# Delta-rule scan in pairs of PSUM banks: one subtraction and one copy for each direction and level, VectorE's other pieces behind the subtraction, and the state's decay on GpSimd

## The chip, the cores and the metric

One core of a Trainium2 chip runs the whole kernel. The metric is the device time of one execution in microseconds (us), lower is better. All data are float32.

## The reference

Two layers of a hybrid trunk over 256 context and 512 latent tokens, width 1024. Each layer projects its normed input, runs three groups of heads (latent attention, a gated delta rule in both directions, pooling), projects back, and then runs an expert-choice mixture of 16 experts. The change lies in the gated delta rule: 4 heads of 128, in two directions.

```python
def gated_delta_chunked(q, k, v, g, beta, s0):
    # chunked: S_t = a_t S_{t-1}(I - b_t k_t k_t^T) + b_t k_t v_t^T, o_t = S_t^T q_t
    gc = jnp.cumsum(chunks(g), axis=-1)
    decay = jnp.exp(jnp.where(incl, gc[..., :, None] - gc[..., None, :], -jnp.inf))
    kb = kc * bc[..., None]
    a_low = jnp.where(strict, jnp.einsum('nbhcd,nbhsd->nbhcs', kb, kc) * decay, 0.0)
    tmat = a_low + jnp.eye(C, dtype=f32)
    w = lax.linalg.triangular_solve(tmat, kb * jnp.exp(gc)[..., None], left_side=True, lower=True, unit_diagonal=True)
    u = lax.linalg.triangular_solve(tmat, vc * bc[..., None], left_side=True, lower=True, unit_diagonal=True)
    qk = jnp.einsum('nbhcd,nbhsd->nbhcs', qc, kc) * decay
    def step(s, inp):
        v_new = u_i - jnp.einsum('bhcd,bhde->bhce', w_i, s)
        o = jnp.einsum('bhcd,bhde->bhce', qg_i, s) + jnp.einsum('bhcs,bhse->bhce', qk_i, v_new)
        s = s * jnp.exp(gl_i)[..., None, None] + jnp.einsum('bhcd,bhce->bhde', kd_i, v_new)
        return s, o
    s_final, o = lax.scan(step, s0.astype(f32), (w, u, qk, qg, kd, g_last))
    ...
```

The decayed state, `s * exp(gl)`, plus the product of a chunk's keys and new values is the state for the next chunk. The triangular solve with `tmat` is what takes the levels below.

## The kernel before

Both layers have the same stages: input projection, attention, the scan of the delta rule (which the change touches), output projection, router, experts. Five engines run their own programs and meet at semaphores: TensorE (`pe`), VectorE (`dve`), ScalarE (`act`), GpSimd (`pool`), and SyncE for the weights' DMAs.

**The scan.** The 768 tokens are six tiles of 128 (`NT`); step `j` (0 to 5) takes tile `j` of the forward direction (`d` = 0) and a tile from the other end for the backward one (`d` = 1), with all four heads. The inverse of a head's 128x128 triangular matrix is built by doubling: after the first blocks (`diagonal_blocks`, L874, and `inverse_of_blocks`, L2226) come five levels `n` = 1 to 5. A level is a chain through three engines:

- `level_factor` (L896): 32 matmuls of 64x64 for both directions, into two banks. Bank `zo` has heads 0 and 1 of both directions, `zd` heads 2 and 3. Both are announced after the last matmuls of direction 1.
- VectorE subtracts each bank from the identity into `gW` (L2288, two instructions of 128x256).
- `level_update` (L914), once for each direction: 32 matmuls into two banks, `x` and `xb`.
- ScalarE copies each of the four banks into the ring's `gXC` (L1795, four instructions of 128x256). The next level's factor reads them; its first matmuls need only `xb` of direction 0.

GpSimd masks the factors' weights for the levels ahead (L2606, L2607, each group counted in the semaphore `ml`).

**The pieces between.** The rest of the rule fills the time in which a level waits. `BETWEEN` gives the pieces of each of 13 slots; TensorE runs slot 2n-1 between factor and update of level n, and slot 2n behind the update:

```python
BETWEEN = (
    (("wt", 0), ("wt", 1)), (("v", 0), ("v", 1)), (("go", 0),), (("go", 1),), (("st", 0), ("st", 1)),
    (("g", 0),), (("g", 1),), (), (("kk", 0),), (("kv", 0),), (("kk", 1), ("qk", 0)), (("qk", 1),), (("kv", 1),))
```

`wt`, `v`, `go`, `st` finish step j-1 (new values, output, state); `g`, `kk`, `qk` prepare step j+1; `kv` transposes the keys and values of step j (`kr` and `vr`, L815, L816). On TensorE `kk` is L807, `qk` L810, `wt` L821, `v` L831 and L833, `go` L844 and L845, `st` L849, and `g` has nothing. VectorE takes their products out of PSUM in its own program order: both subtractions of level n, then slot 2n-1, then slot 2n. So a piece of slot 2n (`st` of slot 4, `kk` of slot 8) stands ahead of the subtractions of level n+1. `st` is four instructions for each direction (L2206: state times decay plus product), `kk` six (L2168 to L2172), `kv` three (L2182, L2183, L2188), and `g` three (L2155 to L2159). In layer 1 `go` and `qk` are left out for context tiles (steps 0 and 1).

In layer 0 TensorE also makes the modulation of both layers in this stage: six loads (`ar`) in each step. One load's first half (L547) is in an even slot, its second half (L547, then L531) in the next odd slot, just ahead of the update. It keeps one bank from the one to the other, and ScalarE empties it (L1498, L1492).

**The banks.** PSUM has eight banks. `claim` takes the next one in a circle and makes TensorE wait there until its last product was read out; `claim_two` takes two neighbours, does not start at bank 7, and skips banks that are held. A claim stands at the head of a group of matmuls, so everything behind it on TensorE waits too:

```python
while turn[0] % BANKS == BANKS - 1 or turn[0] % BANKS in held or (turn[0] + 1) % BANKS in held:
    turn[0] += 1
b = turn[0] % BANKS
turn[0] += 2
for x in (b, b + 1):
    bank_unused(x)
```

With one bank for each claim, a level of the kernel before takes six banks.

## Time and profile before

| | |
|---|---|
| three timed runs | 1947.01, 1946.89, 1941.97 us; median 1946.89 |
| profiled execution | 1942.07 us, its span 1939.9 us, granted clock 0.977 |
| TensorE busy | 1833.6 us, 95% of the span |
| scan of layer 0 (382 to 616 us) | 234.0 us, TensorE busy 224.24 |
| scan of layer 1 (1386 to 1572 us) | 186.0 us, TensorE busy 154.61 |

Everything but the two scans is untouched. The two scans together are 420 of 1939.9 us. In the views, "PE" is TensorE's matmuls, "DVE" VectorE, "ACT" ScalarE, "POOL" GpSimd. The chain of waits lists what came last, piece after piece in order of time; in it a piece of TensorE lasts until the next one's results begin to come, so a start there can lie some 0.07 us behind the instruction's own.

In the rows by stretch the columns are: stretch, its length, then busy us (x instructions) of PE, PEld (weight load), DVE, ACT and POOL, the granted clock, the DMA engines' busy share, and GB/s.

### The profile page before, as it was taken

The numbers are of one execution on the slowest core, as the hardware profiler recorded it, in microseconds if no ns is written. First come the engines' busy times: TensorE is split into PE (matmuls) and PEld (weight loads), VectorE is DVE, ScalarE is ACT, GpSimd is POOL, SyncE is SP. The second block draws the span as 40 slices with busy tenths as digits, with TensorE's granted clock in tenths as the row PEclk, the third lists the DMA queues.
The fourth block names the chain that finished last, engine by engine and source line by source line (L and its number), as shares of the span: only waits on it lengthen the run. The fifth ranks groups of instructions, "written<-read, shape, count | busy, mean of one in ns | idle before, by whom it ended". The sixth has DMA issues, their size and how long they took to land.

```text
span 1939.9 us, 41539 instructions
## 1 busy us (share of the span) xinstructions
PE 1833.6 (95%) x17621; PEld 1150.2 (59%) x17621; DVE 729.0 (38%) x1523; ACT 500.7 (26%) x1133; POOL 376.8 (19%) x506
## 2 busy tenths in 40 slices
PE   6999999999999998999999999999888899999998
PEld 4565556677787554565556445556577764455454
DVE  3145333444553335111121425334465632522323
ACT  3212532343332223001111231353433221200010
POOL 1612000244452001310011032200254610100000
PEclk7999999999999999999999999999899999999999
DMA  9410000164555316889998412000300022499996
GB/s 323 142 57 22 22 1 1 47 212 154 181 172 163 136 44 233 307 330 366 359 364 312 148 44 66 22 0 1 99 14 25 13 89 74 173 411 411 410 411 253
DMA packets 139545, 320.67 MB, mean 165 GB/s; under 512 B 10760, under 2 KB 97582, under 8 KB 124046
## 3 DMA queue, kind: packets, MB, share of 16 engines
q1 hardware_dynamic: 127584, 287.20, 40.0%
q0 software_dynamic: 6432, 20.00, 3.7%
q10 hardware_dynamic: 5390, 11.44, 1.7%
q8 instruction: 110, 1.80, 0.4%
q14 instruction: 29, 0.24, 0.0%
HBM read 305.45 MB, written 13.16 MB: 164 GB/s over the span
## 4 chain that ended last, share of the span: by engine, by line
PE 84%; DVE 6%; issue 4%; ACT 3%; DMA 2%; SPq 1%; POOL 0%; ACTq 0%; DVEq 0%; POOLq 0%
PE psum L610 17%; PE psum L1143 11%; PE psum L1045 7%; PE psum L1174 6%; PE psum L730 3%; PE psum L1152 3%; PE psum L914 3%; PE psum L1224 3%; PE psum L547 2%; PE psum L751 2%; PE psum L896 2%; PE psum L1186 2%; PE psum L807 1%; PE psum L531 1%; PE psum L831 1%
## 5 line engine op out<-in xcount | busy, mean ns | idle before, releaser
L610 PE MATMUL psum<-hT,ring 128*128 128x256 f32 (+2 forms) x976 | 337.7, 503 | 4.3 <-ACT hT L1518 3.8
L610 PEld LDWEIGHTS psum<-hT,ring 128*128 128x128 f32 (+1 forms) x976 | 184.4, 191 | 145.3 <-issue 127.6
L1143 PE MATMUL psum<-ring,arena 128*64 128x256 f32 x1536 | 174.9, 384 | 5.8 <-issue 2.0
L1143 PEld LDWEIGHTS psum<-ring,arena 128*64 128x64 f32 x1536 | 111.1, 138 | 66.6 <-issue 17.4
L1045 PE MATMUL psum<-hT,ring 128*128 128x512 f32 (+1 forms) x384 | 139.4, 521 | 0.9 <-DVE xT L2323 0.9
L2410 DVE TENSOR_TENSOR arena<-arena,psum 128x384 f32<-128x384 f32 (+1 forms) x32 | 15.6, 488 | 260.7 <-PE psum L1152 161.6
L1045 PEld LDWEIGHTS psum<-hT,ring 128*128 128x128 f32 x384 | 72.7, 190 | 64.8 <-issue 61.5
L914 PE MATMUL psum<-wbuf,ring 64*64 64x64 f32 x1920 | 78.4, 229 | 31.3 <-DVE wbuf L2288 25.6
L1795 ACT COPY ring<-psum 128x256 f32<-128x256 f32 x240 | 73.4, 383 | 97.4 <-PE psum L914 97.4
L914 PEld LDWEIGHTS psum<-wbuf,ring 64*64 64x64 f32 x1920 | 68.9, 141 | 37.9 <-issue 35.8
L2717 POOL DMA_INDIRECT big<-h_rows_lat,idx x16 | 15.7, 979 | 381.7 <-PE psum L1248 173.7
L2439 DVE SCALAR_TENSOR_TENSOR xT<-psum,modraw,xT 128x512 f32<-128x512 f32 (+1 forms) x136 | 79.7, 622 | 21.2 <-PE psum L1224 15.1
L730 PE MATMUL psum<-hT,ring 128*128 128x256 f32 (+1 forms) x192 | 82.0, 537 | 0.0
L1863 ACT COPY arena<-psum 128x512 f32<-128x512 f32 (+2 forms) x49 | 23.6, 482 | 220.5 <-PE psum L1165 147.2
L914 PE MATMUL psum<-ring,wbuf 64*64 64x64 f32 x1920 | 75.8, 229 | 0.6 <-issue 0.6
L2067 DVE SCALAR_TENSOR_TENSOR big<-psum,cols,big 128x511 f32<-128x511 f32 (+1 forms) x44 | 27.6, 628 | 125.9 <-ACT big L1619 124.9
L1224 PE MATMUL psum<-arena 128*128 128x512 f32 x144 | 65.8, 602 | 4.0 <-DVE arena L2426 2.3
L1867 ACT ACTIVATE arena<-psum 128x384 f32<-128x384 f32 (+1 forms) x32 | 14.1, 439 | 213.9 <-PE psum L1152 108.6
L914 PEld LDWEIGHTS psum<-ring,wbuf 64*64 64x64 f32 x1920 | 65.0, 141 | 0.7 <-issue 0.7
L2288 DVE TENSOR_TENSOR wbuf<-lev,psum 128x256 f32<-128x256 f32 x120 | 45.1, 418 | 52.0 <-PE psum L896 51.7
L547 PE MATMUL psum<-ring,scol 128*32 128x256 f32 x768 | 64.5, 424 | 0.0
L2606 POOL TENSOR_TENSOR mlaw<-dT,lev 128x256 f32<-128x256 f32 x60 | 43.8, 730 | 104.6 <-PE psum L896 97.0
(351 smaller groups left out, 3386.7 us busy)
## 6 DMA issues: line engine op xcount, KB each, us to landing
ring<-in_moe_w_gate SPq DMA_DIRECT2D x64, 1024.0 KB, 10.9
ring<-in_ada_w SPq DMA_DIRECT2D x48, 1024.0 KB, 5.4
ring<-in_moe_w_up SPq DMA_DIRECT2D x32, 1024.0 KB, 9.1
hT<-in_moe_w_down SPq DMA_DIRECT2D x24, 1024.0 KB, 12.2
ring<-in_w_in SPq DMA_DIRECT2D x20, 1024.0 KB, 6.5
big<-in_moe_w_up SPq DMA_DIRECT2D x16, 1024.0 KB
sz<-in_moe_w_down SPq DMA_DIRECT2D x16, 1024.0 KB
big<-in_moe_w_down SPq DMA_DIRECT2D x16, 1024.0 KB, 14.4
```

The source lines that it names most:

```text
L547: m = pe.matmul(ada[1][r:r + 32, 0:SLOT_COLS], lhsT=scol[:, 2 * k:2 * k + 32], rhs=ada[2][:, k, :], start=half == 0, stop=half == 1)
L610: m = pe.matmul(b[0:c1 - c0, 0:n], lhsT=w[:, k, c0:c1], rhs=hT[:, k, t0:t0 + n], start=k == 0, stop=k == KD - 1)
L730: x = pe.matmul(b[:, 0:n], lhsT=w[:, k, m % 2 * P:(m % 2 + 1) * P], rhs=hT[:, k, t0:t0 + n], start=k == 0, stop=k == KD - 1)
L914: m = pe.matmul(bs[kind][o, i * HALF:(i + 1) * HALF], lhsT=v if transposed else w, rhs=w if transposed else v, start=True, stop=True)
L1045: m = pe.matmul(b[:, 0:x], lhsT=w[:, k, c:c + P], rhs=mixT[:, k, t0:t0 + x], start=k == OUT_REST[0], stop=k == OUT_GDN[-1])
L1143: m = pe.matmul(b[e * CAP_L:(e + 1) * CAP_L, 0:2 * P], lhsT=xs[:, k, e, 0:CAP_L], rhs=w[e][:, 2 * (k - ks[0]) + q, :], start=k == 0, stop= ...
L1152: m = pe.matmul(b[r:r + CAP_C, 2 * P:3 * P], lhsT=xs[:, k, e, CAP_L:CAP], rhs=v[:, 2 * (k % (KD // 2)) + q, f * P:(f + 1) * P], start=k == ...
L1174: m = pe.matmul(ys[c][e * CAP_L:(e + 1) * CAP_L, :], lhsT=hidT[:, q, f * P + e * CAP_L:f * P + (e + 1) * CAP_L], rhs=w[e][:, f, c * 512:(c ...
L1224: m = pe.matmul(b[:, 0:SEQ], lhsT=ylat[:, k * P:(k + 1) * P], rhs=Sl[:, :], start=True, stop=True)
L1795: read_out(act.copy(gXC[j % 2][:, d, w:w + GH, :].rearrange("p h c -> p (h c)"), b), key)
L2288: read_out(dve.tensor_tensor(gW[:, :, h0:h0 + 2, :], eyes, b, ALU.subtract), key)
L2439: read_out(dve.scalar_tensor_tensor(out=x, in0=b[:, 0:n], scalar=mods_of[l][:, 5 * KD + k, 1 - g:2 - g], in1=x, op0=ALU.mult, op1=ALU.add) ...
```

## The change

- A factor is now one group of 16 matmuls for each direction, into a pair of neighbouring banks, announced by itself (`z`). An update also goes into one pair. A level takes eight banks in place of six.
- VectorE subtracts once for each direction (still two instructions of 128x256 for a level, each over two banks). ScalarE copies once for each direction (two of 128x512 in place of four of 128x256).
- VectorE's slot 2n stands behind the subtractions of level n+1 (ahead of slot 2n+1).
- The state's decay is taken off VectorE's `st`: GpSimd multiplies the state by its decay (`decay_state`, one instruction for each direction), between the masks of level 3 and those of level 4, and signals `sdec`. VectorE then adds the product in one instruction for each direction.
- ScalarE issues the loads of the next decay rows at slots 2 and 3, one each, in place of both at slot 4.

```diff
@@ -387,6 +387,12 @@
             product_ready(eng, ("s", l, i, h))
             b = where[("s", l, i, h)][0]
             return psum[:, b:b + 2, :].rearrange("p a c -> p (a c)")[:, 0:(CT if i < CT else NT) * P]
+
+        def two_banks(eng, key):
+
+            product_ready(eng, key)
+            b = where[key][0]
+            return psum[:, b:b + 2, :]
 
         def attended(eng, l, calls, n):
 
@@ -876,34 +882,29 @@
                                 if (d, i) == (1, 1):
                                     done(m, keys[kind])
 
-                def level_factor(j, n, x):
-
-                    keys = ("zo", l, j, n), ("zd", l, j, n)
-                    bs = [claim(key) for key in keys]
-                    for d in range(2):
-                        if n > 1:
-                            evacuated(pe, ("xb", l, j, d, n - 1))
-                        elif d == 0:
-                            evacuated(pe, ("t0o", l, j))
-                            evacuated(pe, ("t0d", l, j))
-                        for i, pair in enumerate(((0, 3), (1, 2))):
-                            if i and n > 1:
-                                evacuated(pe, ("x", l, j, d, n - 1))
-                            for kind, h in enumerate(pair):
-                                c = (2 * d + h % 2) * HALF
-                                for k in range(2):
-                                    t, o = rows_of[k ^ xt_half(h, n)], rows_of[k ^ x_half(h, n)]
-                                    m = pe.matmul(bs[kind][o, c:c + HALF], lhsT=gML[n % 2][t, d, h, :],
-                                                  rhs=x[t, d, XTB[h], :], start=True, stop=True)
-                                if d and i:
-                                    done(m, keys[kind])
+                def level_factor(j, n, x, d):
+
+                    key = ("z", l, j, n, d)
+                    bs = claim_two(key).rearrange("p (a c) -> p a c", a=2)
+                    if n > 1:
+                        evacuated(pe, ("x", l, j, d, n - 1))
+                    elif d == 0:
+                        evacuated(pe, ("t0o", l, j))
+                        evacuated(pe, ("t0d", l, j))
+                    for pair in ((0, 3), (1, 2)):
+                        for kind, h in enumerate(pair):
+                            c = h % 2 * HALF
+                            for k in range(2):
+                                t, o = rows_of[k ^ xt_half(h, n)], rows_of[k ^ x_half(h, n)]
+                                m = pe.matmul(bs[o, kind, c:c + HALF], lhsT=gML[n % 2][t, d, h, :],
+                                              rhs=x[t, d, XTB[h], :], start=True, stop=True)
+                    done(m, key)
 
                 def level_update(j, n, x, d):
 
-                    keys = ("x", l, j, d, n), ("xb", l, j, d, n)
-                    bs = [claim(key) for key in keys]
-                    for kind in range(2):
-                        evacuated(pe, ("zd" if kind else "zo", l, j, n))
+                    key = ("x", l, j, d, n)
+                    bs = claim_two(key).rearrange("p (a c) -> p a c", a=2)
+                    evacuated(pe, ("z", l, j, n, d))
                     same, other = ((2, 1), (0, 0), (1, 0), (2, 0)), ((3, 0), (3, 1), (0, 1), (1, 1))
                     for i in range(GH):
                         for kind, (h, transposed) in enumerate((same[i], other[i])):
@@ -911,10 +912,9 @@
                                 a = rows_of[k ^ x_half(h, n)]
                                 o = rows_of[k ^ (xt_half(h, n + 1) if transposed else x_half(h, n + 1))]
                                 w, v = gW[a, d, h, :], x[a, d, XB[h], :]
-                                m = pe.matmul(bs[kind][o, i * HALF:(i + 1) * HALF], lhsT=v if transposed else w,
+                                m = pe.matmul(bs[o, kind, i * HALF:(i + 1) * HALF], lhsT=v if transposed else w,
                                               rhs=w if transposed else v, start=True, stop=True)
-                            if i == GH - 1:
-                                done(m, keys[kind])
+                    done(m, key)
 
                 def first_chunk(n):
 
@@ -980,7 +980,8 @@
                     gdn_between(j, 0)
                     for n in range(1, LEVELS - 1):
                         pe.wait_ge(s["ml"], (LEVELS - 1) * j + n + 1)
-                        level_factor(j, n, x)
+                        for d in range(2):
+                            level_factor(j, n, x, d)
                         gdn_between(j, 2 * n - 1)
                         if n == 1:
                             pe.wait_ge(s["x0"], j + 1)
@@ -990,7 +991,6 @@
                     keys = ("z6d", l, j), ("z6o", l, j)
                     bs = [claim(key) for key in keys]
                     for d in range(2):
-                        evacuated(pe, ("xb", l, j, d, LEVELS - 2))
                         evacuated(pe, ("x", l, j, d, LEVELS - 2))
                     for i in range(2):
                         for kind, h in enumerate((i, 2 + i)):
@@ -1722,9 +1722,8 @@
                             gdn_piece(what, i, d)
                     if slot in G_SLOTS and j + 1 < NT:
                         gdn_piece("g", j + 1, G_SLOTS.index(slot))
-                    if slot == 4 and 1 <= j < NT - 1:
-                        for d in range(2):
-                            decay_rows(j + 1, d)
+                    if slot in (2, 3) and 1 <= j < NT - 1:
+                        decay_rows(j + 1, slot - 2)
                     if l == 0 and slot % 2 and slot < 2 * ADA_CHUNK:
                         ada_out(ADA_FIRST + ADA_CHUNK * j + slot // 2)
                     if j == 0 and slot < 4:
@@ -1789,10 +1788,9 @@
                     for n in range(1, LEVELS - 1):
                         gdn_between(j, 2 * n - 1)
                         for d in range(2):
-                            for w, name in ((GH, "xb"), (0, "x")):
-                                key = (name, l, j, d, n)
-                                b = product_ready(act, key)[:, 0:GH * HALF]
-                                read_out(act.copy(gXC[j % 2][:, d, w:w + GH, :].rearrange("p h c -> p (h c)"), b), key)
+                            key = ("x", l, j, d, n)
+                            b = two_banks(act, key)[:, :, 0:GH * HALF]
+                            read_out(act.copy(gXC[j % 2][:, d, :, :].rearrange("p (a h) c -> p a (h c)", a=2), b), key)
                         gdn_between(j, 2 * n)
                     for w, name in ((0, "z6d"), (2, "z6o")):
                         key = (name, l, j)
@@ -2202,11 +2200,9 @@
                         if j == 0:
                             read_out(dve.tensor_copy(S[:, d, :, :].rearrange("p h c -> p (h c)"), b), key)
                         else:
-                            for h in range(GH):
-                                m = dve.scalar_tensor_tensor(out=S[:, d, h, :], in0=S[:, d, h, :],
-                                                             scalar=gt4[:, j % 2, d, 1, h:h + 1],
-                                                             in1=b[:, h * P:(h + 1) * P], op0=ALU.mult, op1=ALU.add)
-                            read_out(m, key)
+                            dve.wait_ge(s["sdec"], 2 * (j - 1) + d + 1)
+                            x = S[:, d, :, :].rearrange("p h c -> p (h c)")
+                            read_out(dve.tensor_tensor(x, x, b, ALU.add), key)
 
                 def gdn_between(j, slot):
 
@@ -2280,14 +2276,15 @@
                 for j in range(NT):
                     if j:
                         inverse_of_blocks(j)
-                    gdn_between(j, 0)
                     for n in range(1, LEVELS - 1):
-                        for h0, name in ((0, "zo"), (2, "zd")):
-                            key = (name, l, j, n)
-                            b = product_ready(dve, key)[:, 0:GH * HALF].rearrange("p (d h c) -> p d h c", d=2, h=2)
-                            read_out(dve.tensor_tensor(gW[:, :, h0:h0 + 2, :], eyes, b, ALU.subtract), key)
+                        for d in range(2):
+                            key = ("z", l, j, n, d)
+                            b = two_banks(dve, key)[:, :, 0:2 * HALF].rearrange("p a (h c) -> p a h c", h=2)
+                            read_out(dve.tensor_tensor(gW[:, d, :, :].rearrange("p (a h) c -> p a h c", a=2), eyes, b,
+                                                       ALU.subtract), key)
+                        gdn_between(j, 2 * n - 2)
                         gdn_between(j, 2 * n - 1)
-                        gdn_between(j, 2 * n)
+                    gdn_between(j, 2 * LEVELS - 4)
                     gdn_between(j, 2 * LEVELS - 3)
                     key = ("u6", l, j)
                     b = product_ready(dve, key)[:, 0:GH * HALF].rearrange("p (h c) -> p h c", h=GH)
@@ -2608,8 +2605,8 @@
 
                 def mask_read(j, n):
 
-                    product_ready(pool, ("zo", l, j, n))
-                    product_ready(pool, ("zd", l, j, n))
+                    for d in range(2):
+                        product_ready(pool, ("z", l, j, n, d))
 
                 def begin(j):
 
@@ -2633,6 +2630,17 @@
                     product_ready(pool, ("t0d", l, j))
                     pool.wait_ge(s["x0"], j + 1)
                     masked(2, j)
+
+                def decay_state(j):
+
+                    for d in range(2):
+                        if need_ctx or tile_of(d, j) >= CT:
+                            product_ready(pool, ("go", l, j, d))
+                        else:
+                            product_ready(pool, ("v", l, j, d))
+                        x = S[:, d, :, :]
+                        pool.tensor_tensor(x, x, gt4[:, j % 2, d, 1, :].unsqueeze(2).to_broadcast([P, GH, P]), ALU.mult
+                                           ).then_inc(s["sdec"], 1)
 
                 def queries(j):
 
@@ -2658,10 +2666,11 @@
                     for n in range(3, LEVELS - 1):
                         mask_read(j, n - 2)
                         masked(n, j)
+                        if n == 3 and j >= 2:
+                            decay_state(j - 1)
                     if j + 1 < NT:
                         decays(j + 1)
                     for d in range(2):
-                        evacuated(pool, ("xb", l, j, d, LEVELS - 2))
                         evacuated(pool, ("x", l, j, d, LEVELS - 2))
                         if j:
                             product_ready(pool, ("v", l, j - 1, d))
```

## Rows read from the trace of the kernel before

**Rows 1.** Busy time by stretch: scan of layer 0, its step 4, scan of layer 1.
```profile
382.00:616.00 234.00, 224.24 (x4673) 176.85 (x4672) 115.64 (x276) 88.08 (x264) 100.64 (x129) 0.97 0.57 184
...
541.66:581.23 39.57, 38.86 (x812) 31.48 (x816) 21.14 (x53) 13.76 (x44) 18.25 (x24) 1.00 0.54 176
...
1386.00:1572.00 186.00, 154.61 (x3864) 138.12 (x3861) 108.78 (x266) 70.09 (x192) 91.57 (x119) 0.95 0.09 28
```

**Rows 2.** Waits in the scan of layer 1: total us, times, longest.
```profile
PE psum L914 <- DVE wbuf L2288: 24.4, 21, 1.6
```

**Rows 3.** Waits in the scan of layer 0.
```profile
PE psum L914 <- issue: 5.9, 5, 2.8
```

**Rows 4.** Chain of waits, layer 1, step 5: levels 3 to 4. Start, us, what.
```profile
1563.23 1.16 PE psum L914 x64
...
1564.53 1.09 PE psum L896 x30
...
1565.64 0.76 DVE wbuf L2288 x2
...
1566.54 1.16 PE psum L914 x64
```

**Rows 5.** Timeline of ScalarE, layer 1, step 5, level 3.
```profile
1564.01 1.20 ACT L1795 COPY ring<-psum 128x256 f32<-128x256 f32 x4 [4.04 <-PE psum L914]
```

**Rows 6.** Timeline of VectorE, layer 1, step 3, levels 3 to 5.
```profile
1493.46 2.16 DVE L2206 SCALAR_TENSOR_TENSOR arena<-arena,small,psum 128x128 f32<-128x128 f32 x8 [1.49 <-PE psum L849]
1495.54 0.75 DVE L2288 TENSOR_TENSOR wbuf<-lev,psum 128x256 f32<-128x256 f32 x2
...
1502.03 0.42 DVE L2168 TENSOR_TENSOR dT<-psum,arena 64x256 f32<-64x256 f32 x1 [2.43 <-PE psum L807]
...
1504.30 0.75 DVE L2288 TENSOR_TENSOR wbuf<-lev,psum 128x256 f32<-128x256 f32 x2
```

**Rows 7.** Chain of waits, layer 1, step 3: `st`, factor 3, and from update 4 on.
```profile
1492.34 1.98 PE psum L849 x16
1494.32 0.69 PE psum L896 x31
...
1499.74 1.16 PE psum L914 x64
...
1505.20 1.16 PE psum L914 x64
```

**Rows 8.** Chain of waits, layer 0, step 4: levels 1, 2, 3 and 5.
```profile
550.33 1.27 PE psum L914 x64
...
557.87 1.09 PE psum L914 x64
...
561.51 0.62 PE psum L896 x32
...
563.24 1.09 PE psum L914 x64
...
564.90 0.71 issue
...
570.22 0.83 PE psum L896 x32
...
573.18 1.27 PE psum L914 x64
```

**Rows 9.** Timeline of ScalarE, layer 0, step 4.
```profile
543.41 0.60 ACT L1707 ACTIVATE arena<-psum 128x512 f32<-128x512 f32 x1 [2.91 <-PE psum L821]
...
550.64 0.17 ACT L1492 COPY modraw<-psum 128x4 f32<-128x4 f32 x1
```

**Rows 10.** Timeline of VectorE, layer 0, step 4.
```profile
542.78 0.68 DVE L2188 TENSOR_TENSOR arena<-psum,small 128x512 f32<-128x512 f32 x1
```

**Rows 11.** Groups by line in the scan of layer 1: busy us, mean ns; idle before.
```profile
L1795 ACT COPY ring<-psum 128x256 f32<-128x256 f32 x120 | 36.2, 385 | 83.4 <-PE psum L914 83.4
...
L2585 POOL TENSOR_TENSOR arena<-arena,small 128x512 f32<-128x512 f32 x10 | 10.4, 1041 | 29.3 <-ACT arena L1704 29.3
```

More of the change, by code:

```diff
@@ L338, in build_program @@
                  "lmul", "egc", "xg", "dex", "eb", "dm", "x0", "xd", "away", "ml", "qg", "osq", "mixd", "rmax",
-                 "rexp", "aff", "top", "hrow", "att", "tok", "idx", "gath", "grow", "gr0", "gr1", "cur", "scat", "arow", "S", "dve", "pool_e"]
+                 "rexp", "aff", "top", "hrow", "att", "tok", "idx", "gath", "sdec", "grow", "gr0", "gr1", "cur", "scat", "arow", "S", "dve", "pool_e"]
         FIRST_ALONE = ("zero", "zrow", "scat", "arow")
```

## The prediction

> **What bounds the kernel now.** I read the page's busy time, then busy time by stretch, then in both scans the chain of waits and the timelines of each engine, and last I followed the claims of PSUM banks through the code.
>
> The reader should see two different stages under one code. In layer 0 the scan lasts 234.0 us and TensorE is busy for 224.24 of them; in its step 4 it is 38.86 of 39.57 [rows 1]. The loads of the modulation and the pieces fill every wait of a level, so a shorter chain through VectorE and ScalarE gains next to nothing there, and each new wait of TensorE is paid in full. In layer 1, without those loads, it is busy for 154.61 of 186.0 us [rows 1], and 24.4 us of its idle time end with VectorE's subtraction [rows 2]. Only there can the change gain.
>
> **A level that nothing fills** (layer 1). From update 3 to update 4 of step 5 it is 1566.54 - 1563.23 = 3.31 us [rows 4]: copies begin 0.78 behind the update's start [rows 4, 5], the factor goes on until the last copy is out (1.09 in place of 0.69 [rows 4, 7]), two subtractions take 0.76, and 0.14 passes to TensorE [rows 4]. With the change, S being the update's start: half an update is 0.54 of 1.09 us [rows 8], so direction 0 is still ready at S+0.78. Its one copy of 128x512 takes 0.60, the time of a ScalarE read of this size [rows 9]; factor 0 starts at S+1.52, 16 matmuls are 0.31 (half of 0.62 [rows 8]) and ready at about S+2.0, one subtraction is 0.42, update 0 starts at S+2.56. Direction 1 is copied by S+1.92, its factor ends at S+2.37, its subtraction at about S+2.95, just in time behind update 0. Gain 0.75 us.
>
> The wide copy itself gains little: the four narrow ones take 1.20 together [rows 5] though one takes 385 ns [rows 11], so they overlap and two take some 0.65, against 0.60. The Trainium skill (VectorE: DVE Perf Modes, The TRN2 errata) gives ScalarE a fixed cost for each instruction, 172 cycles at 1.2 GHz out of PSUM, paid once by a large tile; by it a merged pair would save an estimated 0.14 us at each of the about nine levels on the path of layer 1, so 1.3 us more than I forecast. The rows agree with its duration of one instruction, not with a saving in a row of them.
>
> **What the banks do.** This is the part on which the sign hangs. A level now takes 8 of 8 banks, before 6. Following both kernels' claims in program order: before, no claim meets a bank whose user is fewer than seven claims back. Now these meet young ones, each at the head of TensorE's queue:
> - update 5, direction 0, takes the bank of `kk` of slot 8 (steps 0 to 4, both layers), which VectorE now reads behind both subtractions;
> - update 3 takes the banks of `st` (steps 1 to 5), also read behind them. In layer 1 direction 1 waits for both. In layer 0 direction 0 waits for both in steps 2, 3 and 5, where bank 7 is skipped, and the directions for one each in steps 1 and 4;
> - in layer 0 updates 1 and 5 (direction 0) take the bank of the load that TensorE ended just ahead of them; update 2 so in steps 2 and 5, and its direction 1 in steps 0, 1, 4; direction 1 of update 4 in all, of update 3 in step 0.
>
> **Layer 1, step 3, summed.** Factor 3 starts at 1494.32 [rows 7]. Before, eight instructions of `st` of 2.16 us stand ahead of the subtractions, which begin at 1495.54 [rows 6]. Now: subtractions from about 1494.8 to 1495.5, then two adds of 0.68 [rows 10] that overlap a little, to 1496.7. Update 3, direction 1, starts at 1496.85 (direction 0 is long done), its copy is out at 1498.23, its factor at 1498.7, its subtraction at 1499.3, so update 4 ends at 1499.99, against 1499.74 + 1.09 = 1500.83 before [rows 7, 8]. 0.84 gained. `kk` follows on TensorE. Factor 5 starts at 1501.1, the subtractions end at 1502.3, then `kk` on VectorE, 1504.30 - 1502.03 = 2.25 [rows 6], then the bank: update 5 at 1504.67 against 1505.20 [rows 7]. So 0.53 is left, and VectorE, busy from there to the step's end, hands on the same 0.53. Steps 1 and 2 have no `go` behind update 1, hence one unfilled level more: 0.53 + 0.75 = 1.3 each. Step 4: 0.53. Step 5 has no `kk`, and 0.8 stays; its last level is filled by `kv`. Step 0, where ScalarE's gates hold the first levels, about 1.0. Sum 1.0 + 2.6 + 1.1 + 0.8 = **5.5 us gained** in layer 1.
>
> **Layer 0, summed**, on step 4's rows.
> - Update 1: the load's last read-out ends at 550.81 [rows 9]; with 0.14 direction 0 starts at 550.95, not 550.33. Before, only the last bank of direction 1 was shared with the load, and the update took 1.27, not 1.09 [rows 8]: that proves the kind of wait and its price of 0.18, which goes. Net 0.5, steps 1 to 5: 2.5.
> - Update 2: 0.7 in steps 2 and 5, 0.16 where it is direction 1 (three): 1.9.
> - Update 3: factor at 561.51 [rows 8], the first subtraction at 561.9, the second ends 562.7, adds until 563.9, start 564.03, not 563.17: 0.86 in three steps; 0.3 in steps 1 and 4, 0.16 in step 0: 3.4.
> - Update 4: 0.16 six times: 1.0.
> - Update 5: factor at 570.22 [rows 8], subtractions until 571.4, `kk` 2.25 to 573.6, start 573.74, end 574.83, before 573.18 + 1.27 = 574.45 with its start counted 0.07 late: 0.45 five times, and 0.5 for the load in step 5: 2.8.
>
> Together 11.6 us. Not all adds: TensorE already stands without cause in the semaphores, 5.9 us in updates [rows 3], 0.71 once ahead of factor 4 [rows 8]. A stop may take such a stall's place. I take 2 us off; the bounds are 0 and 8 (5.9 and some more of the 234.0 - 224.24 us idle). **9.6 us lost.**
>
> **Costed at nothing.** VectorE saves 2.16 - 1.3 us of `st` in each step; in layer 1 this is in the sum, in layer 0 also. GpSimd's two decays are 1.04 each by the same form [rows 11] and wait for `go` of slot 3; behind them stand the masks of level 4, two instructions of half that size, for which factor 4 waits. `go` ends as update 2 begins, 1492.34 - 1.09 = 1491.25, and update 4 starts at 1499.74 [rows 7, 8], factor 4 some 2 us ahead of it: 6.4 us of room for 2.1 + 1.0. `st` on VectorE waits for `sdec`; its product comes 1.09 + 1.98 = 3.1 us behind `go`'s [rows 7, 8]. Without this cover each microsecond would be paid in five steps. The decay rows' loads go earlier on ScalarE, some 0.4 us of issue each, and wait for `go`, which is done before update 2's copies: nothing. Two-bank reads on either engine: nothing, bound 0.05 us for each on the path, some 2 us.
>
> **Sum.** 9.6 - 5.5 = +4.1 us. On the profiled execution's 1942.07 (span 1939.9) this is 1946.2. That execution lies 4.8 below the median of the runs, 1946.89, two of which stand within 0.12 of each other. On the median: **1951.0 us**.
>
> **Rivals.**
> - *The waits of layer 0 cost nothing.* If its pace is set by what TensorE's sequencer waits for without a semaphore [rows 3], stops merely take the place of those stalls. With all 9.8 us of idle time [rows 1] as cover: 11.6 - 9.8 - 5.5 = -3.7, 1943.2. Against it: update 1's 1.27 [rows 8], where a shared bank was paid in full. It decides the sign from 11.6 - 5.5 = 6.1 us absorbed.
> - *Faster, by the shorter level.* If the subtraction ahead of the pieces is worth the whole of its wait in layer 1, as it is where no bank is shared, then of the 24.4 us that end with it [rows 2] about half go (0.75 of each 1.5), 12 us, while layer 0, spared by the same, keeps the load's waits, 2.5 + 1.9 + 1.0 = 5.4: 5.4 - 12 = -6.6, 1940.3. It needs `kk` and `st` out of their banks before updates 5 and 3, though VectorE starts them later than before. It decides from a layer 1 that gains more than layer 0 loses.
> - *The stops feed on each other.* ScalarE's `g` activations (three of 128x512, so 1.8 us [rows 9]) then stand ahead of the load's read-out and of the copies of level 4, another 0.5 us in ten steps, with nothing absorbed: 11.6 + 5 - 5.5 = +11, 1958.
> - *GpSimd's masks come late.* If `decay_state` holds factor 4: over 3 us of cover must go; 1 us in eight steps is +8 on the forecast, 1959.
>
> **Chances.** Forecast (0 to +8 us) 0.52; waits absorbed (-6 to 0) 0.20; faster by over 6 us 0.10; stops feed on each other 0.14; masks 0.04. The likeliest one's own range is 1947 to 1955. The range for 8 in 10 reaches into both sides: 1940 to 1959. 0.3% is 5.8 us, about what a measurement of this kernel can tell from no change: faster 0.13, same 0.50, slower 0.37.
>
> **What would show it.** Right: the scan of layer 0 some 8 to 10 us longer with TensorE's busy time the same, stops of 0.5 to 0.9 ahead of updates 1, 3 and 5, the last two ended by VectorE's `st` and `kk`; the scan of layer 1 some 5 shorter, an unfilled level at 2.6 us; the idle time ended by L2288 well below 24.4. Wrong: layer 0 unchanged, or `ml` waits ahead of factor 4.

## The result, and the profile after

The changed kernel takes 1953.57 us (median of 6 runs, 1951.23 to 1959.29), the kernel before, timed beside it, 1945.61 (6 runs, 1936.59 to 1947.01). The ratio, estimated from all runs, is 1.0058, with a 95% interval of [1.0043, 1.0074], so 8 to 14 us slower; the two medians alone are 8.0 us apart, a quotient of 1.0041. The predicted 1951.0 and its range hold, but the loss is over the 0.3% that a measurement can tell, to which I gave 0.37 against 0.50 for no change. The profiled execution's span is 1950.0 us against 1939.9: 10.1 more, where the forecast was 4.1.

In the changed kernel's lines, L899 is the factor, L915 the update, L2283 the subtraction, L1793 the copy, L2166 to L2170 `kk` on VectorE, L2205 `st`'s add, L553 and L537 the modulation's load, L1492 its read-out. First, busy time by stretch, both whole scans (from their first factor to the output projection), before the change:

```profile
385.32:626.12 240.80, 230.90 (x4745) 184.87 (x4742) 117.53 (x278) 86.79 (x265) 99.69 (x129) 0.97 0.55 179
1389.36:1585.25 195.89, 163.89 (x3953) 148.46 (x3953) 112.18 (x270) 70.22 (x194) 93.16 (x123) 0.95 0.07 23
```

and after it:

```profile
382.07:636.94 254.87, 230.98 (x4744) 183.30 (x4741) 114.38 (x254) 82.72 (x205) 107.65 (x137) 0.97 0.52 169
1402.89:1595.61 192.72, 161.88 (x3953) 145.92 (x3953) 109.50 (x246) 66.94 (x134) 101.50 (x131) 0.96 0.07 24
```

Layer 0 is 14.1 us longer with TensorE's busy time unchanged (230.90 and 230.98): all of it is standing still. Layer 1 is 3.2 shorter. The stages around the scans differ by -3.2, +2.7 and -0.3. TensorE's waits in layer 0, which answer to [rows 3]:

```profile
PE psum L915 <- issue: 12.4, 11, 2.8
PE psum L915 <- ACT modraw L1492: 3.6, 5, 0.7
PE psum L915 <- DVE ring L2170: 3.2, 5, 0.7
PE psum L915 <- DVE arena L2205: 2.3, 3, 0.8
PE psum L553 <- issue: 1.3, 1, 1.3
```

The main bank waits foretold are there: the load's read-out ahead of update 1 in five steps, `kk` ahead of update 5 in five, `st` ahead of update 3 in steps 2, 3 and 5. The first row was not foretold: "issue" in updates, a stop for which the trace names no semaphore, has doubled from [rows 3]. Six of its eleven stops are of 0.9 us or more, 10.3 us in all. The other five are of 0.57 or 0.18 us, 2.1 us in all, and each ends 0.09 or 0.10 us behind a read-out of the load's bank or of `st`, at places foretold ahead of updates 2, 3 and 5. They are bank waits as well. Layer 1, to be held against [rows 2]:

```profile
PE psum L915 <- DVE ring L2170: 7.0, 4, 1.8
PE psum L899 <- ACT ring L1793: 6.6, 10, 2.0
PE psum L915 <- issue: 3.8, 4, 1.7
PE psum L915 <- DVE wbuf L2283: 3.6, 12, 0.6
PE psum L915 <- DVE arena L2205: 3.1, 4, 0.8
```

The subtraction's 24.4 us have shrunk to 3.6, yet only 3.2 us came out: `kk`'s and `st`'s banks took much of the place. The fifth wait for `kk`'s bank, in step 1, is in the "issue" row (1.71 us, ending 0.10 behind `kk`'s last read-out), and the factors now wait 6.6 us for ScalarE's copies, 1.6 before. The chain of waits of layer 1's step 3, to be held against [rows 7] (start, us, what):

```profile
1505.39 0.44 PE psum L899 x15
...
1506.52 0.69 DVE arena L2205
...
1507.89 0.73 PE psum L915 x31
...
1512.25 0.43 PE psum L899 x15
...
1515.32 0.30 DVE ring L2170
...
1515.66 1.16 PE psum L915 x64
```

From factor 3, the update starts 2.50 us later (I had 2.53), factor 5 is 6.86 later (6.78), update 5 10.27 (10.35; before 10.88). VectorE's timeline there answers to [rows 6]:

```profile
1505.85 0.75 DVE L2283 TENSOR_TENSOR wbuf<-lev,psum 128x256 f32<-128x256 f32 x2 [2.80 <-PE psum L899]
1506.52 1.28 DVE L2205 TENSOR_TENSOR arena<-arena,psum 128x512 f32<-128x512 f32 x2
...
1512.70 0.75 DVE L2283 TENSOR_TENSOR wbuf<-lev,psum 128x256 f32<-128x256 f32 x2 [1.63 <-PE psum L899]
1513.38 0.41 DVE L2166 TENSOR_TENSOR dT<-psum,arena 64x256 f32<-64x256 f32 x1
```

`st` went from 2.16 to 1.28 us, but stands between subtraction and update, whose bank it frees. The unfilled level of step 5, in the chain, answers to [rows 4]:

```profile
1575.85 0.73 PE psum L915 x31
1576.58 0.02 issue
1576.60 0.59 ACT ring L1793
...
1577.33 0.50 PE psum L899 x16
...
1577.85 0.43 DVE wbuf L2283
...
1578.41 0.59 PE psum L915 x25
```

1578.41 - 1575.85 = 2.56 us from update to update, against 3.31 before. This looks like the 2.56 forecast, but both rows are of direction 1, which `st`'s bank had held back; the forecast was of direction 0, whose updates start at 1574.36 and 1577.58, 3.22 apart. A level as short as forecast shows only in e3 below (2.49). Layer 0's step 4, to be held against [rows 8]:

```profile
551.71 0.07 ACT modraw L1492
551.78 0.25 issue
552.03 1.16 PE psum L915 x64
...
571.62 0.38 PE psum L899 x12
...
575.03 0.30 DVE ring L2170
575.33 0.04 issue
575.38 1.16 PE psum L915 x64
...
579.08 1.34 issue
580.42 0.59 PE psum L553 x2
```

Update 1 waits for the load's read-out, update 5 for `kk`, 3.76 us behind factor 5's start (2.96 before, 3.52 foretold; where nothing else disturbs the step it is 3.49, and 2.75 or 2.76 before). Then TensorE stands 1.34 us inside a load with no semaphore named.

### The profile page after: what moved, and what is told of

The parts are those of the page before. It is cut to its first block, busy times and chain, and to the rows that moved or that the text cites. A ratio compares the mean times of both kernels' runs of the same rounds, so it can differ in the third digit from the quotient of the medians.

```text
span 1950.0 us, 41394 instructions
## 1 busy us (share of the span) xinstructions
PE 1824.5 (94%) x17621; PEld 1140.5 (58%) x17621; DVE 723.1 (37%) x1475; ACT 492.8 (25%) x1013; POOL 392.6 (20%) x522
## 4 chain that ended last, share of the span: by engine, by line
PE 82%; DVE 7%; issue 4%; ACT 3%; DMA 3%; SPq 1%; POOL 0%; ACTq 0%; DVEq 0%; POOLq 0%
PE psum L616 17%; PE psum L1143 11%; PE psum L1045 7%; PE psum L1174 5%; PE psum L915 3%; PE psum L736 3%; PE psum L1152 3%; PE psum L1224 3%; PE psum L757 2%; PE psum L553 2%; PE psum L899 2%; PE psum L1186 2%; PE psum L813 1%; PE psum L837 1%; PE psum L789 1%
## 5 line engine op out<-in xcount | busy, mean ns | idle before, releaser
L915 PE MATMUL psum<-wbuf,ring 64*64 64x64 f32 x1920 | 78.7, 228 | 38.4 <-issue 14.2
L2283 DVE TENSOR_TENSOR wbuf<-lev,psum 128x256 f32<-128x256 f32 x120 | 46.6, 419 | 160.5 <-PE psum L899 160.2
L1793 ACT COPY ring<-psum 128x512 f32<-128x512 f32 x120 | 66.4, 587 | 112.2 <-PE psum L915 112.0
L915 PEld LDWEIGHTS psum<-wbuf,ring 64*64 64x64 f32 x1920 | 68.4, 139 | 43.3 <-issue 23.3
L2436 DVE SCALAR_TENSOR_TENSOR xT<-psum,modraw,xT 128x512 f32<-128x512 f32 (+1 forms) x136 | 79.7, 620 | 21.2 <-PE psum L1224 14.1
L915 PE MATMUL psum<-ring,wbuf 64*64 64x64 f32 x1920 | 76.4, 228 | 2.0 <-issue 2.0
L915 PEld LDWEIGHTS psum<-ring,wbuf 64*64 64x64 f32 x1920 | 64.9, 139 | 5.2 <-issue 5.2
L553 PE MATMUL psum<-ring,scol 128*32 128x256 f32 x768 | 62.5, 407 | 5.2 <-DMA ring<-in_ada_w 3.6
L2112 DVE TENSOR_REDUCE small<-psum 128x1 f32<-128x768 f32 (+1 forms) x40 | 33.8, 850 | 80.5 <-PE psum L757 80.3
```

Source lines behind the costliest of these rows:

```text
L553: m = pe.matmul(ada[1][r:r + 32, 0:SLOT_COLS], lhsT=scol[:, 2 * k:2 * k + 32], rhs=ada[2][:, k, :], start=half == 0, stop=half == 1)
L915: m = pe.matmul(bs[o, kind, i * HALF:(i + 1) * HALF], lhsT=v if transposed else w, rhs=w if transposed else v, start=True, stop=True)
L1793: read_out(act.copy(gXC[j % 2][:, d, :, :].rearrange("p (a h) c -> p a (h c)", a=2), b), key)
L2283: read_out(dve.tensor_tensor(gW[:, d, :, :].rearrange("p (a h) c -> p a h c", a=2), eyes, b, ALU.subtract), key)
L2436: read_out(dve.scalar_tensor_tensor(out=x, in0=b[:, 0:n], scalar=mods_of[l][:, 5 * KD + k, 1 - g:2 - g], in1=x, op0=ALU.mult, op1=ALU.add) ...
```

## The experiments

The changed kernel was timed beside before (1945.61). Of the experiments, the first four ran on one chip (before: 1940.47 us, median of 29 runs), the next four on a second (1939.95, 17 runs), the last three on a third (1944.59, 11 runs). Scan lengths are from one execution of each; the ratios are estimated from all runs and differ a little from the quotients of the medians.

| kernel | median us | ratio to before, 95% | layer 0 | layer 1 |
|---|---|---|---|---|
| before | | 1 | 240.8 | 195.9 |
| changed | 1953.57 | 1.0058 [1.0043, 1.0074] | 254.9 | 192.7 |
| e1 pairs only | 1944.07 | 1.0014 [0.9995, 1.0032] | 255.3 | 185.2 |
| e2 order, decay only | 1937.20 | 0.9983 [0.9967, 0.9999] | 243.3 | 193.3 |
| e3 in place | 1916.90 | 0.9882 [0.9856, 0.9909] | 231.3 | 182.3 |
| e4 changed, old order | 1938.56 | 0.9991 [0.9970, 1.0011] | 251.5 | 185.1 |
| e5 changed, 128 waits | 1951.19 | 1.0050 [1.0034, 1.0066] | 249.5 | 194.8 |
| e6 in place, old order | 1918.62 | 0.9885 [0.9861, 0.9908] | 236.9 | 181.9 |
| e7 in place, pairs only | 1923.57 | 0.9919 [0.9897, 0.9941] | 233.4 | 185.0 |
| e8 before, 128 waits | 1935.85 (1 run) | | 238.9 | 196.4 |
| e9 in place, `kk` first | 1928.86 | 0.9919 [0.9898, 0.9941] | 235.6 | 186.8 |
| e10 changed again | 1954.35 (1 run) | | 252.7 | 196.2 |
| e11 changed, 64 waits | 1955.99 (1 run) | | 257.6 | 194.8 |

**e1, the pairs alone.** VectorE's order, `st` of four instructions and the place of the decay rows' loads as before the change:

```diff
+                    gdn_between(j, 0)
                     for n in range(1, LEVELS - 1):
...
-                        gdn_between(j, 2 * n - 2)
                         gdn_between(j, 2 * n - 1)
-                    gdn_between(j, 2 * LEVELS - 4)
+                        gdn_between(j, 2 * n)
...
-                        if n == 3 and j >= 2:
-                            decay_state(j - 1)
```

> Only the bank pairs (one subtraction and one copy for each direction); VectorE's order, the four-instruction st and the decay rows' loads as before. My theory (young banks in TensorE's claims cost layer 0; the level itself is shorter in layer 1): layer 0's scan is 8 to 10 us longer, by stops ahead of updates 1, 2 and 5 that end with the read-out of the modulation load, none that end with st or kk; layer 1's scan 6 to 8 us shorter; the ratio to before 0.999 to 1.003. Rival (the reordering is what costs): ratio under 0.998, layer 0 within 3 us of before.

Layer 0's loss is the pairs' own (+14.5, where I had 8 to 10), but layer 1 gains 10.7 (I had 6 to 8), far more than with the whole change: without the new order the trace names no wait on `kk` or `st` in either layer.

**e2, order and decay alone**, on banks by twos of a level's halves as before:

```diff
-                    gdn_between(j, 0)
                     for n in range(1, LEVELS - 1):
...
+                        gdn_between(j, 2 * n - 2)
                         gdn_between(j, 2 * n - 1)
-                        gdn_between(j, 2 * n)
+                    gdn_between(j, 2 * LEVELS - 4)
```

> Only VectorE's pieces behind the subtraction, the decay on GpSimd and the earlier loads of the decay rows; one bank for each claim, as before. My theory: layer 0's scan within 2 us of before, layer 1's 2 to 4 us shorter (update 3 some 0.5 us sooner in five steps, update 5 not, since its direction 1 takes kk's bank); ratio 0.997 to 1.000. Rival (the reordering or GpSimd's decay is what costs): layer 0 some 5 us longer or more, ratio over 1.002.

It is a little faster than before (layer 0 is 2.5 us longer, layer 1 2.6 shorter). The halves alone give +0.14 and -0.17%, together +0.58: what they lose together is neither's own. In layer 1 TensorE stands 1.39 or 1.40 us at one place of each of five steps, 7.0 us in all, for which the trace names no semaphore. The place tells the cause:

```profile
1503.32 0.29 DVE L2171 TENSOR_TENSOR ring<-psum,arena 64x128 f32<-64x128 f32 x1
...
1503.72 0.27 PE L914 MATMUL psum<-wbuf,ring 64*64 64x64 f32 x2 [1.39 <-issue]
```

It is update 5 between its two directions, and in all five steps it goes on 0.10 us behind the end of `kk`'s last read-out: the wait for `kk`'s bank that the expectation names. In layer 1 it costs nothing over the kernel before, which stands 1.56 or 1.57 us for the subtraction ahead of the same update in steps 1 to 4: from factor 5 to the next step it is 12.57 us here and 12.59 before.

**e3, the update in the bank pair of its own factor.** Four banks a level in place of eight, everything else as changed. The factor of a direction has been read when its update begins, so the wait is one that the update has anyway.

```diff
                     key = ("x", l, j, d, n)
-                    bs = claim_two(key).rearrange("p (a c) -> p a c", a=2)
                     evacuated(pe, ("z", l, j, n, d))
+                    b0 = where[("z", l, j, n, d)][0]
...
+                    where[key] = (b0, uses[b0], 0)
+                    uses[b0] += 1
+                    second_of[b0 + 1] = (b0, uses[b0])
+                    bs = psum[:, b0:b0 + 2, :]
```

> The changed kernel, but an update takes the pair of banks of its own direction's factor, whose read-out it waits for anyway, so a level takes four banks in place of eight. My theory (the new waits are all of banks): no stop of an update ends with st, kk or a load's read-out, layer 0's scan is within 3 us of before, layer 1's some 12 us shorter, ratio to before 0.992 to 0.995. Rival (order, decay or wide reads cost, whatever the banks): layer 0 stays 8 us or more over before, ratio 1.000 or more.

The banks were the loss, and the gain is larger than expected: 1.2% faster than before. Every wait on `st` and on the load's read-out is gone; of those on `kk` 1.1 us is left in layer 1. Its stretches:

```profile
385.72:617.04 231.32, 225.71 (x4745) 181.18 (x4741) 113.89 (x254) 82.55 (x205) 107.66 (x137) 0.99 0.58 186
1380.13:1562.40 182.27, 159.80 (x3954) 144.28 (x3954) 108.58 (x247) 66.58 (x134) 101.13 (x131) 0.98 0.08 25
```

Layer 0 is 9.5 us under before. In place the load's bank is shared with no update any more (9.14 from factor 1 to factor 2, before 9.32; 10.62 from factor 5 on, before 10.80), some 2 us in all; the rest goes with less standing still (5.6 us against 9.9) and a clock granted at 0.99, not 0.97.

**e4, the changed kernel with VectorE's old order** (the diff of e1 without its last two lines).

> The changed kernel with VectorE's order of before (slot 2n ahead of the subtractions of level n+1); pairs, decay on GpSimd and earlier loads stay. My theory: stops that end with st go, update 5 waits for the load alone; layer 0's scan 8 to 10 us over before, layer 1's 7 to 9 under it, ratio 0.998 to 1.002, so 0.4% better than the changed kernel. Rival (the order gains, as it is meant to): slower than the changed kernel, ratio 1.008 or more.

It is as fast as before and by the ratios 0.67% faster than the change. With eight banks a level, the new order, made to shorten the level, costs more than it gives: TensorE waits 9.4 us for the subtraction in place of 3.6, but no longer for `kk` and `st`.

```profile
PE psum L915 <- DVE wbuf L2284: 9.4, 15, 1.2
PE psum L899 <- ACT ring L1793: 4.3, 7, 2.0
PE psum L915 <- issue: 1.9, 2, 1.4
```

**e6 and e7, the same two on top of the in-place banks.** e6 is e3 with the old order, e7 is e3 with all of e1's diff.

> The in-place kernel (update in the bank pair of its own direction's factor, four banks a level) with VectorE's pieces in their old order around the subtraction. Theory A (the new order is harmful only by holding kk's and st's banks, which nobody young waits for any more with four banks a level): the new order is then worth its price in layer 1, so this kernel is slower than the in-place one by 2 to 5 us there, ratio to before about 0.990. Theory B (the new order gains nothing even so, because the old pieces fitted beside the level): the same as the in-place kernel within 1.5 us, ratio about 0.988.

> The bank pairs alone, in place: VectorE's old order, the state's decay in VectorE's st as before the change, decay rows loaded at the old place. Against the pairs alone with eight banks a level (255.3 us of scan in layer 0, 185.2 in layer 1). Theory A (bank waits are all that the pairs cost): scan of layer 0 at 231 to 236, of layer 1 at 182 to 184, ratio to before 0.988 to 0.991, so the order and GpSimd's decay are worth nothing measurable together. Theory B (in place needs the new order, since the subtraction is what the level waits for): layer 1 at 187 or more, ratio 0.992 or more. Also: GpSimd's masks ended 6.4 us of waits of the diagonal blocks in layer 1 of the in-place kernel; if its two decays of 1.04 us each are the cause, these waits are near 1.5 us here.

e6 equals e3 by the ratio: once no claim meets a young bank, one whose product was claimed just ahead, the order is worth nothing measurable in either direction (Theory B there). e7 falls between its two theories. It is 0.34% slower than e6 by the ratios, whose intervals overlap a little (0.26% by the medians, on one chip); layer 1, by 3.1 us, agrees: an `st` of 2.16 us in place of 1.28 ahead of the subtraction makes factor 3 to factor 4 3.25 us in place of 2.67 in four steps. So GpSimd's decay seems to gain there; the place of the decay rows' loads, which e7 changes too, was not tried alone. The waits for GpSimd ahead of the diagonal blocks, 6.4 us in e3, are 1.3 us in e7, but also in e6, with the decay on GpSimd: the decay is not their cause.

**e9, `kk` of direction 1 ahead of `kv` on VectorE**, on e3:

```diff
                         gdn_between(j, 2 * n - 2)
+                        if n == LEVELS - 2 and j + 1 < NT:
+                            gdn_piece("kk", j + 1, 1)
                         gdn_between(j, 2 * n - 1)
-                    gdn_between(j, 2 * LEVELS - 4)
+                    if j + 1 < NT:
+                        gdn_piece("qk", j + 1, 0)
```

> The in-place kernel with VectorE's kk of direction 1 ahead of kv of direction 0, nothing else. In layer 1 of the in-place kernel the levels are down to 2.49 us, but 6.4 us of TensorE's waits (five of some 1.3) end with GpSimd's mask ahead of the diagonal blocks, and those masks wait for kk of direction 1, which VectorE begins 1.15 us late behind three instructions of kv of 0.68 each. Theory A (this queue is the end of a step): the five waits fall to 0.3 or so each, the scan of layer 1 from 182.3 to 177 to 179 us, the ratio to before 0.985 to 0.987. Theory B (VectorE as a whole bounds the step, so the order of its pieces moves the wait elsewhere): scan of layer 1 at 181 to 183, ratio as the in-place kernel's, 0.988.

Neither theory held: the ratio is 0.9919, and layer 1 grew to 186.8 us. 1.4 of the 4.5 us between it and e3 is a stop of the kind below, in step 1. The waits moved. The three largest of e3 in layer 1, then the three that are new in e9 (its waits for ScalarE's copies are 6.4 us, for the subtraction 3.4):

```profile
PE psum L899 <- ACT ring L1798: 7.5, 10, 2.7
PE psum L880 <- POOL mlaw L2609: 6.4, 5, 2.6
PE psum L920 <- DVE wbuf L2288: 3.3, 12, 0.6
```

```profile
PE psum L827 <- DVE ring L2301: 3.3, 5, 0.8
PE psum L821 <- DVE arena L2186: 2.5, 4, 0.6
PE psum L880 <- DVE arena L2191: 1.6, 1, 1.6
```

GpSimd's masks no longer end a wait, VectorE's other pieces do. The reason can be read in e3's own chain, which from the end of step 3 into step 4 runs on VectorE for 9.0 us (1485.49 to 1494.51) with no other engine in it:

```profile
1485.83 0.69 DVE arena L2185
1486.52 0.60 DVE arena L2186
1487.12 0.60 DVE arena L2191
1487.72 0.32 DVE dT L2171
...
1489.87 1.27 DVE arena L2180 x2
```

So in the in-place kernel VectorE's queue sets the end of a step of layer 1, and there a shorter level, now 2.49 us, should not help.

**e5, e8, e10 and e11: the stops that no semaphore ends.** The "issue" rows needed a cause. Here is the longest, the chain of the changed kernel in layer 0's step 0, and then the DMA queues of the same kernel from 396.5 to 397.7 us (packets, MB, share of 16 engines):

```profile
396.14 2.83 issue
398.97 0.35 PE psum L915 x9
```

```profile
q8 instruction: 1, 0.02, 5.4%
```

This one packet of the instruction queue took 0.054 x 16 x 1.2 = 1.04 us; by its record it ended at 397.60, and TensorE went on 1.37 behind. e5, e8 and e11 put the same wait, long fulfilled, 128, 128 and 64 times into TensorE's program, and e10 is the changed kernel itself once more:

```diff
                 pe.wait_ge(s_const, 16 * CONST_DMAS)
+                if l == 0:
+                    for _ in range(128):
+                        pe.wait_ge(s_const, 16 * CONST_DMAS)
```

> The changed kernel with 128 waits more on TensorE (each on a semaphore that has long reached its value) ahead of layer 0's attention, nothing else. In the traces so far every stop of TensorE of 0.9 us or more in the scan of layer 0 that no semaphore ends is over 1.2 to 1.4 us behind the landing of a 16 KB packet of the instruction queue; before these stops sum to some 6 us in layer 0's scan, with the change to some 11.7. The extra instructions move the borders of those packets by half a packet against the program. Theory A (the stops belong to where a packet's border falls in the program): their places move, and their sum in layer 0's scan changes, to 3 to 9 us, and the scan gets shorter by as much (254.9 to some 248 to 252). Theory B (the new bank waits make TensorE's supply late wherever the borders lie): the sum stays at 10 to 13 us at other places, the scan at 253 to 257. The whole is within 1 us of the changed kernel but for that, the waits themselves under 5 us.

> The kernel before with the same 128 waits more on TensorE ahead of layer 0's attention. Theory A (places of packet borders): the stops of 0.9 us and more without a semaphore, 5.6 us in the scan of layer 0 (1.62, 2.78, 1.17), move to other places and their sum changes, to 2 to 9 us. Theory B (only waits make them): the sum stays at 4 to 7 us.

> The changed kernel itself, profiled once more. If the stops of TensorE that no semaphore ends stand where a packet of the instruction queue lands late in the program, they are at the same places as in its first profile (9.3 and 16 us into step 0, 26 into step 1, 29 in steps 3 and 5, 38 in step 4), with a sum of 10 to 13 us in layer 0's scan; if they come by chance of one execution, the places differ and the sum is anywhere from 5 to 13.

> The changed kernel with 64 waits more on TensorE ahead of layer 0's attention, a quarter of a packet of the instruction queue. So far these stops summed to 3.5 to 6.7 us in the scan of layer 0 of the five kernels without young bank claims, to 7.0 to 12.9 in the four with them. Theory B (bank waits bring more such stops, wherever the borders are): 7 us or more here. Theory A (only the place of the borders decides): 3 to 7 us is as likely as more.

Over all 13 profiles, layer 0's scan has 58 such stops of 0.9 us or more, and every one ends 1.08 to 1.74 us behind the end of such a packet, though these packets come only every 6 us or so (38 in the scan of the changed kernel and of the one before). Their places belong to the program. Counted in matmuls of the trace from the scan's first, those of the changed kernel stand ahead of matmul 218, 343, 1088, 1213, 2827, 3822 and 4441. These numbers differ by multiples of some 124, and 4744 matmuls for 38 packets are 125 for each. e10 has five of the seven, at the same numbers. The five of e11, with 64 waits more, are at 203, 1072, 1197, 2811 and 4425, each 15 or 16 ahead of one of the seven. The five of e5, with 128, fit the same spacing moved by 31: 1057 is 31 ahead of 1088, and 3666 is 31 and once 124 to 125 ahead of 3822. Of e8's three, 2045 is 31 ahead of one of before's (2076). So the packets' borders set the places. The waits moved them by a quarter and an eighth of a packet, not by the half and the quarter that I had expected.

Their lengths vary by execution (sums of 11.65 and 8.29 us for the same kernel, where I had expected 10 to 13 again). And their sum goes with the bank waits: 2.7 to 6.7 us in the seven profiles of kernels that wait little for young banks in this layer (before 5.57, e8 5.12, e2 5.17, e3 2.72, e6 6.71, e7 3.84, e9 4.53), 7.0 to 11.7 in the six that wait for them much (changed 11.65, e10 8.29, e11 8.12, e5 6.99, e1 11.60, e4 9.90). Three pairs of these kernels differ only in taking the update's banks in place, and each time the sum is the smaller: 2.72 against 11.65 and 8.29, 6.71 against 9.90, 3.84 against 11.60. But each is one execution or two, that edit also moves the borders (e3's stops stand at 220 and 4470), and the two groups nearly meet at 6.71 and 6.99. The expected ranges don't decide it either: e5 came out in Theory A's for the sum and the scan (249.5 us), e11 in Theory B's, e8 in both. That bank waits raise the sum is likely and not proven, and why they would stays open.

## Why the prediction was right in its range and too low

Factor-to-factor times carry the whole comparison (us; layer 0: the undisturbed value of steps 2 to 5, layer 1: step 3):

| stretch | before | changed | in place (e3) |
|---|---|---|---|
| layer 0, factor 1 to 2 | 9.32 | 9.94 | 9.14 |
| layer 0, factor 2 to 3 | 7.36 | 8.00 (steps 2, 5), 7.35, 7.48 | 7.35 |
| layer 0, factor 3 to 4 | 3.39 | 4.24 (steps 2, 3, 5), 3.72 | 3.39 |
| layer 0, factor 4 to 5 | 4.54 | 4.67 | 4.56 |
| layer 0, factor 5 to the step's end | 10.80 | 11.35 | 10.62 |
| layer 1, factor 3 to 4 | 3.48 | 3.06 | 2.49 |
| layer 1, factor 4 to 5 | 4.19 | 3.80 | 3.29 |
| layer 1, factor 5 to the step's end | 9.59 | 9.78 | 9.27 |

- **Update 1 and the load's bank** (2.5 us forecast): 0.62 in five steps, 3.1.
- **Update 2** (1.9): 0.64 twice and 0.1 in step 4, 1.4.
- **Update 3 behind `st`** (3.4; 0.86 each): 0.85 in three steps, 0.33 in step 4, about 3.2.
- **Update 4** (1.0; 0.16 each): 0.13 in step 4, so 0.8.
- **Update 5 behind `kk` and the load** (2.8): 0.55 five times and 0.57 in step 5, 3.3.
- **The sum of layer 0** was 11.6 and comes out at 11.8, in part by luck: the five terms are off by 0.2 to 0.6 us each, and cancel. The step that failed is the next one, "I take 2 us off", because a stop might take a stall's place. TensorE's idle time in this scan grew by 14.0 us, from 9.9 to 23.9. The bank waits at the places foretold are 11.2 of it. The kernel before had 4.3 us of shorter idle times, of which 1.0 is left, so 3.4 were absorbed, and that part of the step was right in kind. But the stops of 0.9 us or more without a semaphore, which I had counted only as cover, grew by 6.1 us (5.57 to 11.65; by 2.7 in e10). 11.2 - 3.4 + 6.1 = 13.9: the step's net is +2.7 us where I had -2, and layer 0 lost 14.1 (11.9 in e10), not 9.6.
- **Layer 1** (5.5 gained): steps 3 and 0 gained 0.63 and 1.45, against 0.53 and 1.0. Steps 1 and 2 gave 0.4 and 0.6 in place of 1.3 each, step 4 lost 1.8 in place of gaining 0.53, step 5 gained 1.9 in place of 0.8. In steps 0, 2 and 4 there are now stops behind such a packet (0.98, 0.73, 0.51, 0.59), where the kernel before has none in this layer; behind the last and a wait of 1.77 us for `kk`'s bank, TensorE's granted clock fell to 0.5, its lower level of 1.2 GHz, for 3.41 us, and factor 5 to the next step took 14.28 us for 12.78. That is most of what steps 2 and 4 lack: the same unforeseen term, and the clock. Step 1 has no such stop. It took 0.19 us more than before from factor 1 to factor 2, 0.21 more in level 3 and 0.53 more from factor 5 on, with `kk`'s bank, where I had counted no loss; why the three grew stays open. In e10 layer 1 gains nothing (196.2).
- **The sign.** e1 and e4 show what the forecast had right in kind and placed wrongly: not the pairs but the pairs with the new order lose. I had priced both waits of `kk` and `st` and still counted the order as part of the gain.
- **Costed at nothing**: two-bank reads, rightly (60 copies of 128x512 over two banks have a mean of 586 ns, against the 0.60 us of one bank [rows 9]; VectorE's subtraction 419 ns for 418), the loads' move, and the decay behind `go`. The one wait for `ml` that the trace names ahead of factor 4 is of 0.89 us of a weight load in step 0 of layer 1, where no decay runs, and it ends 0.8 us behind the mask and 1.5 behind a packet. By e7 the decay is a gain, if anything.
- **ScalarE's fixed cost.** 60 wide copies were busy for 33.3 us in layer 1's scan, 120 narrow ones for 36.2 [rows 11]: 2.9 / 60 = 0.05 us saved by a merged pair, the same as my 0.65 - 0.60. The Trainium skill's fixed cost for each instruction (VectorE: DVE Perf Modes, The TRN2 errata), by which it would be an estimated 0.14, doesn't show as such between copies that follow each other.

The rivals: that layer 0's waits cost nothing is refuted by the table; "faster, by the shorter level" needed `kk` and `st` out of their banks, which is what e3 made true, and it gave more than the rival's 6.6; that stops feed on each other has the nearest size (+11, against 10.1 by the spans and 8.0 by the medians) by another mechanism, for from factor 4 to factor 5 the undisturbed time grew by 0.13 us, not by the 0.5 of late copies; late masks did not occur.

## What to carry to other kernels

When an edit makes buffers bigger, follow each claim back to its last reader: a claim that meets one issued just ahead turns that reader's place in its queue into a term of the critical path, and an order that shortens one chain may lengthen just that. Ask first whether the result can go where the operand just consumed lies; here this one edit turned +0.6% into -1.2%. And where an engine has no slack, existing stalls cover new waits only in part (3.4 of 11.2 us here), and may themselves grow.

## What of the hardware was not expected

TensorE's stops of 0.9 us or more without a semaphore, up to 2.83 us, all end 1.1 to 1.7 us behind a 16 KB packet of a DMA queue of kind instruction, and their places move with such packets' borders when waits are added ahead. What fits is that a stream of small matmuls (64x64) in a full layer is held up by the arrival of its own program, for 3 to 12 us in some 240. And after several of these stops the granted clock fell to 0.5 (behind the one that ended at 398.97, from 399.36 on for 3.41 us; behind that of 525.46 to 527.40, from 529.07), so a stop costs more than its length: factor 5 to the next step, into which the second of these fell, took 15.38 us for 14.53.
